# Where the memory keys' projection runs, and how the early low parts and gated attention's steps are spread

## The reference, cut to what matters

```
block 1: z = rmsnorm([meta; x]) @ w_in -> a, q, k, v, r, lr, ga, gb
         y_a = multiscale_pool(a) mixed per group @ w_pool_out
         o   = gated linear attention over chunks of 64 (q, k, v, decay from lr), normed, * silu(r)
         m   = sigmoid(ga) * y_a + sigmoid(gb) * (o @ w_gla_out);  h += m @ w_out
         h  += squared_relu(rmsnorm(h) @ w_ff1) @ w_ff2
block 2: p = rms_norm(x) @ w_in_first -> a depthwise convolution of width 31 and an 8-head
             recurrence (rwkv7), concatenated, @ w_out
         cross attention: q = h @ wq; km, vm = split(rms_norm(mem) @ wkv);  mem is 256 x 1024
         a gated MLP (w_gu, w_down)
```

## Time and profile before

| what | value |
|---|---|
| median of 3 runs | 1596.79 us |
| the profiled execution | 1598.76 us, its span 1596.9 us |
| PE busy | 1554.9 us, 97% of the span |
| DVE, ACT, POOL busy | 829.8, 648.1, 376.8 us |
| TensorE clock granted over the span | 0.992 |
| mean DMA traffic | 134 GB/s |

### The profile page before, as it was taken

How to read it: one execution, slowest core, us unless ns; L and a number is a source line. 1 busy time by engine, 2 the same in 40 slices (tenths; PEclk the granted TensorE clock), 3 DMA queues, 4 the chain that set the end, 5 groups by cost and what they waited for, 6 DMA issues and landing times.

```text
span 1596.9 us, 27596 instructions
## 1 busy us (share of the span) xinstructions
PE 1554.9 (97%) x11744; PEld 1279.7 (80%) x11744; DVE 829.8 (52%) x1290; ACT 648.1 (41%) x1019; POOL 376.8 (24%) x319
## 2 busy tenths in 40 slices
PE   8999999999999999999999988999999999999997
PEld 7887778888888888887877777779789888888877
DVE  6887523753455454545477866345427432333334
ACT  5444423443444352543465554444335322322222
POOL 0122211222011010241363251032023420330234
PEclk9999999999999999999999999999999999999999
DMA  6243212333667767634535221145122223232211
GB/s 252 84 142 113 80 54 79 111 126 134 238 245 244 256 240 264 224 108 169 199 120 185 79 105 62 56 182 187 53 80 80 81 104 106 79 106 91 94 63 70
DMA packets 49147, 213.40 MB, mean 134 GB/s; under 512 B 5248, under 2 KB 11008, under 8 KB 34048
## 3 DMA queue, kind: packets, MB, share of 16 engines
q1 hardware_dynamic: 49024, 211.63, 37.7%
HBM read 183.30 MB, written 28.31 MB: 133 GB/s over the span
## 4 chain that ended last, share of the span: by engine, by line
PE 88%; DVE 6%; issue 3%; ACT 1%; POOL 1%; DMA 0%; SPq 0%; POOLq 0%; DVEq 0%; ACTq 0%
PE ps L171 88%; DVE zf L183 2%; DVE zf L191 1%; DVE wl L183 1%; POOL zf L183 1%; DVE zr L191 1%; PE ps L174 1%; DVE ps L191 1%; ACT zf L177 1%; DVE zf L2513 0%; ACT zf L180 0%; ACT wh L180 0%; DMA wl<-lo_scratch 0%; ACT zr L180 0%; DMA zf<-in_xT 0%
## 5 line engine op out<-in xcount | busy, mean ns | idle before, releaser
L171 PE MATMUL ps<-zr,wh 128*128 128x512 f32 (+2 forms) x4028 | 1163.3, 375 | 9.6 <-ACT wh L180 5.7
L171 PEld LDWEIGHTS ps<-zr,wh 128*128 128x128 f32 x4028 | 722.8, 189 | 157.7 <-issue 7.3
L171 PE MATMUL ps<-zr,wl 128*128 128x512 f32 (+2 forms) x2008 | 742.7, 372 | 0.0
L183 POOL TENSOR_TENSOR zf<-zf 128x512 f32<-128x512 f32 (+1 forms) x230 | 271.2, 1186 | 705.3 <-ACT zf L177 478.6
L171 PEld LDWEIGHTS ps<-zr,wl 128*128 128x128 f32 x2008 | 377.7, 189 | 71.5
L183 DVE TENSOR_TENSOR wl<-raw,wh 128x1024 fp32r<-128x1024 f32 (+2 forms) x201 | 246.8, 1267 | 158.9 <-ACT wh L180 158.7
L180 ACT ACTIVATE wh<-raw 128x1024 fp32r<-128x1024 f32 (+2 forms) x243 | 240.5, 1038 | 154.9 <-PE ps L171 141.7
L177 ACT ACTIVATE zf<-zf 128x512 f32<-128x512 f32 (+2 forms) x232 | 128.0, 561 | 356.0 <-DVE zf L183 259.9
L183 DVE TENSOR_TENSOR zf<-ps,zf 128x512 f32<-128x512 f32 (+3 forms) x172 | 98.3, 578 | 178.7 <-PE ps L171 152.7
L171 PE MATMUL ps<-zf 64*64 64x64 f32 (+5 forms) x4024 | 150.7, 240 | 19.1 <-issue 8.7
L171 PEld LDWEIGHTS ps<-zf 64*64 64x64 f32 (+3 forms) x4024 | 113.2, 141 | 58.5 <-issue 41.2
(11 more groups left out here) (91 smaller groups left out, 633.3 us busy)
## 6 DMA issues: line engine op xcount, KB each, us to landing
raw<-in_wstream SPq DMA_DIRECT2D x116, 1024.0 KB, 5.3
zf<-in_wstream SPq DMA_DIRECT2D x42, 512.0 KB, 4.9
lo_scratch<-zr SPq DMA_DIRECT2D x42, 512.0 KB, 4.8
wl<-lo_scratch SPq DMA_DIRECT2D x42, 512.0 KB, 4.1
zf<-in_xT SPq DMA_DIRECT2D x16, 256.0 KB, 3.8
raw<-in_wstream SPq DMA_DIRECT2D x4, 768.0 KB, 4.3
x_scratch<-zf SPq DMA_DIRECT2D x8, 256.0 KB, 2.1
zf<-x_scratch SPq DMA_DIRECT2D x8, 256.0 KB, 4.9
```

The costliest lines, as they stand in the source:

```text
L171: return self.raw.matmul(out_, l, x, start=start, stop=stop)
L183: return self.raw.tensor_tensor(out_, a, b, o)
```

## The change

1. The four units of km move in the stream of weights from behind v to behind vm. In `schedule()` their eight tiles are gone from block 1; `bg_mem2` does them after the last packet of vm, as 32 packets of 6 matmuls (`mk`, two of a tile's eight k each), with the letter m, which `TURNS` now has 78 times for 41. `TURNS` is written anew. The normalised memory that vm is made from serves km too, so its first high and low parts (`mem.x` on ACT and DVE) go; the squares stay.
2. The four pooling mixes move among the tiles of the second unit of v.
3. `EARLY` takes km's eight pieces in and drops the two of the third unit p (the condition looks 4 units back, not 2). There are 48 pieces; piece p is read at step p, split at p + 3, and written at p + 4, so `int(1.15 * p)` is `p`.
4. Gated attention's steps: gb's tiles get rate 4 for 2. Extra empty steps: one before the scores of level 4, two before those of level 5, and more among the norms.
5. The outcome of the convolution goes to other buffers (`CR`), so it no longer waits for vm's last tile, but for the last `prep`. `wa` waits for km. The reciprocal root of the memory's norm is spread behind vm. km's results go to DRAM tile by tile (128 KB), not in pairs.

```diff
@@ unit_list
-    pair("km", "wkv_2", 0, 4)
...
     for i in range(4):
         t("vm", "wkv_2", 0, 8, (1024 + 256 * i,), 256, "M")
+    pair("km", "wkv_2", 0, 4)
@@
-EARLY = [... if u[0] in ('cv', 'vm', 'wa', 'wb', 'wq') or u[0] == "p" and UNITS[n - 2][0] in ("p", "cv")]
+EARLY = [... if u[0] in ('cv', 'vm', 'km', 'wa', 'wb', 'wq') or u[0] == "p" and UNITS[n - 4][0] in ("p", "cv")]
@@ bg_gla
+            for _ in range((4, 5, 5).count(lv)):
+                yield
...
             put("gla.sq", h)
             yield
+            if h:
+                yield
             pl.cols(f"gla.n{h}", "M")
             yield
-            if h in (0, 3):
-                yield
+            yield
@@ schedule
-            if uu == 0 and i == 2:
-                pl.spread("mem.rs")
+            if uu == 1:
+                pl.drain(bgp)
+                pl.take("M", "in.mx", i)
+                put("mix", i)
+                pl.rel("M", "in.mx", i)
         mark("v", uu)
-    pl.drain(bgp)
-    for uu in range(4):
-        n = pl.next_unit("km")
-        for j in range(2):
-            ...
-            pl.tile(n, j, 2 * uu + j)
...
-    pl.rate = 2
-    for tag, cnt in (("r", 2), ("ga", 4), ("gb", 4)):
+    for tag, cnt, pl.rate in (("r", 2, 2), ("ga", 4, 2), ("gb", 4, 4)):
@@ early
-                if int(1.15 * p) == t - 4:
+                if p == t - 4:
                     put("early.out", p)
...
-                if int(1.15 * p) == t:
+                if p == t:
                     put("early.in", p)
...
-                if int(1.15 * p) == t - 3:
+                if p == t - 3:
                     put("early", p)
@@ bg_conv
-        while not has(("vm", 3, 1)):
+        while not has(("vm", 3, 1), ("prep", 3)):
@@ bg_mem2
+        pl.spread("mem.rs", "M")
+        yield
+        for uu in range(4):
+            n = pl.next_unit("km", ahead=False)
+            pl.split(n + 1)
+            pl.load(n + 2)
+            yield
+            for j in range(2):
+                i = 2 * uu + j
+                pl.take("D", "t.km", i)
+                for k in range(0, 8, 2):
+                    put("mk", n, j, i, k, k + 2)
+                    if k == 6:
+                        put("ev.km", i)
+                        pl.rel("D", "t.km", i)
+                        mark("km", uu, j)
+                    yield
@@ bg_out
-        while not has(("conv",), ("vm", 3, 1)):
+        while not has(("conv",), ("km", 3, 1)):
@@ scalar, mem_x
-                e.cp(mem_hl(k)[0], mem_src(k), scale=vec("mem_norm_g_2", k)).then_inc(*e.up("mem.h", k))
@@ vector
-            def mem_x(k):
-                e.wait_ge(("mem.rs.sq", k))
-                lo_scaled(("mem.x", k), mem_hl(k)[1], mem_src(k), vec("mem_norm_g_2", k), mem_hl(k)[0], "mem.h", k)
```

More of the change, by code:

```diff
@@ L22 @@
 TURNS = """
[L23 to L27, removed]
+...p.pp.p.p.....pg.pgpp.g.pp.gcppcccgcgcgcpgc.gcggg.cccgcc.cpgcg.hhg.g.gcc.hgg.g.gghchc.hhcphgg.hgpc
+hgpphcc.cgcgg.g.hcp.gphpchghccg.ccmggccg..cppp.pghch.h.mphccphmphmcmphcmpcimmipmmffmpmpicicmifpmimim
+pfgciccmmcgifficmfccpmifmpmfifpgimmicmpcmgmmgccgpmcipmmpmfpmfphcmhfmgpcmmcfhpimmmificghihgcmhggigphi
+chccgmimhhfmggmmgffmccfmhgfpmmpmmhfmmgcmgchgchfpmfhpmfphmpfcpcpmfcmpmccmfmpmmfiimhifmcifhmhihcmihimc
+mciihffmfifmcmfmimfmcfcicfmoifoifiooofififfioofiifiofiofooofffffofofofoofofofofoofofooofofooooooooo
 """
@@ L113 @@
 UNITS = unit_list()
-EARLY = [n for n, u in enumerate(UNITS) if u[0] in ('cv', 'vm', 'wa', 'wb', 'wq') or u[0] == "p" and UNITS[n - 2][0] in ("p", "cv")]
+EARLY = [n for n, u in enumerate(UNITS) if u[0] in ('cv', 'vm', 'km', 'wa', 'wb', 'wq') or u[0] == "p" and UNITS[n - 4][0] in ("p", "cv")]
 PIECES = [(n, c) for n in EARLY for c in range(2)]
@@ L522, in schedule @@
                 pl.cols("mem.rs")
-            if uu == 0 and i == 2:
-                pl.spread("mem.rs")
-        mark("v", uu)
-    pl.drain(bgp)
-    for uu in range(4):
-        n = pl.next_unit("km")
-        for j in range(2):
[L530 to L533, removed]
-            pl.tile(n, j, 2 * uu + j)
+            if uu == 1:
[3 more added lines that the diff above has]
+                pl.rel("M", "in.mx", i)
+        mark("v", uu)
     for uu in range(2):
@@ L1133, in program @@
         U = sb("cu_sb", [P, NCU], u8)
-        mh = sb("mh", [P, 8, 16])
+        MR = sb("mr", [P, 256])[:, :]
+        mh, sm, km16 = MR[:, 0:128].rearrange("p (k t) -> p k t", t=16), MR[:, 128:192], MR[:, 192:256]
         msq = sb("msq", [P, 16])
         mrs = sb("mrs", [P, 16])
-        sm = sb("sm", [P, 64])
-        km16 = sb("km16", [P, 64])
         x_raw_m = mh
@@ L1243, in program @@
         ACC, TMP, RSTD, TMP2 = F(66), F(67), F(68), F(69)
-        RA, MR = F(63), F(38)[:, 256:512]
+        RA = F(63)
         cu_raw, pmx = F(55, NCU), F(54)
@@ L1256, in program @@
         mraw = F(0, 2048)
-        kv_out = [F(73), F(74), F(50)]
+        km_out = [F(40)[:, 0:256], F(40)[:, 256:512]]
         vm_out = [F(51)[:, 256:512], F(40)[:, 0:256]]
@@ L1283, in program @@
         ZC = [F(47, 2168)[:, 542 * i:542 * (i + 1)] for i in range(4)]
-        CS = [64, 44, 22, 23]
+        CS, CR = [64, 44, 22, 23], [38, 39, 49, 50]
         CO, CP = [F(i) for i in CS], F(58)
@@ L1324, in cat_hl @@
         def cat_hl(i):
-            return R(CS[i]), R(47 + i)
+            return R(CS[i]), R(CR[i])
         def prep_bufs(hp):
@@ L1437, in operand @@
                 return R(RO[k]), R(VS[k]), ("fin.out", k)
-            if tag == "km":
-                return (*mem_hl(k), ("mem.x", k))
-            if tag == "vm":
+            if tag in ("vm", "km"):
                 return (*mem2_hl(k), ("mem.x2", k))
@@ L1500, in mm, with mk @@
                 for k in range(nk // 2) if half == 0 else range(nk // 2, nk):
-                    dense(n, j, ps(*K), k, operand(tag, i, k), 256 if tag == "km" else 512, K)
+                    dense(n, j, ps(*K), k, operand(tag, i, k), 512, K)
+            def mk(n, j, i, k0, k1):
+                K = ("t.km", i)
+                if k0 == 0:
+                    e.wait_ge(freed(*K))
+                for k in range(k0, k1):
+                    dense(n, j, ps(*K), k, operand("km", i, k), 256, K)
             def part(n, j, i, k, h):
@@ L1589, in ko @@
                         e.wait_ge(freed(*K))
-                    dense(n, j, ps(*K), k, operand(tag, i0 + j, k), 256 if tag == "km" else 512, K)
+                    dense(n, j, ps(*K), k, operand(tag, i0 + j, k), 512, K)
             def rows(n, i, name, k0=0, k1=8):
@@ L1972, in tensor @@
             run(e, {
-                "mm": mm, "idle": idle, "lr": lr, "mw": mw, "kw": kw, "kt": kt, "ko": ko, "mh": mh, "koh": koh, "rows": rows, "cols": cols, "spread": spread, "gla.gate": gla_gate,
+                "mm": mm, "idle": idle, "lr": lr, "mw": mw, "kw": kw, "kt": kt, "ko": ko, "mh": mh, "koh": koh, "mk": mk, "rows": rows, "cols": cols, "spread": spread, "gla.gate": gla_gate,
                 "gla.score": gla_score, "gla.turn": gla_turn, "gla.turnm": gla_turnm, "gla.state0": gla_state0,
@@ L2268, in cat @@
                 e.wait_ge(("conv.res", i))
-                e.cp(cat_hl(i)[0], F(47 + i)).then_inc(*e.up("cat.h", i))
+                e.cp(cat_hl(i)[0], F(CR[i])).then_inc(*e.up("cat.h", i))
             def ev_wa(i):
@@ L2658, in conv_out @@
             def conv_out(i):
-                e.wait_ge(("conv.sg", i), ("conv.x", i), ("mm", "t.vm", pl.base["vm"][3], 1))
-                e.stt(F(47 + i), CO[i], vec("conv_ln_b_2", i), F(45 + i % 2), ADD, MUL).then_inc(*e.up("conv.res", i))
+                e.wait_ge(("conv.sg", i), ("conv.x", i))
+                e.stt(F(CR[i]), CO[i], vec("conv_ln_b_2", i), F(45 + i % 2), ADD, MUL).then_inc(*e.up("conv.res", i))
             def pset():
@@ L2816, in cat @@
             def cat(i):
-                lo(("cat", i), cat_hl(i)[1], F(47 + i), cat_hl(i)[0], "cat.h", i)
+                lo(("cat", i), cat_hl(i)[1], F(CR[i]), cat_hl(i)[0], "cat.h", i)
             def ev_wb(i):
@@ L2826, in evh_wb @@
                 e.tt(half(YS[i], h), half(ps("t.wb", i), h), half(WP[i], h), ADD).then_inc(*e.up(*K))
-            def mem_x(k):
-                e.wait_ge(("mem.rs.sq", k))
-                lo_scaled(("mem.x", k), mem_hl(k)[1], mem_src(k), vec("mem_norm_g_2", k), mem_hl(k)[0], "mem.h", k)
             def mem_x2(k):
                 lo_scaled(("mem.x2", k), mem2_hl(k)[1], mem2_src(k), vec("mem_norm_g_2", k), mem2_hl(k)[0], "mem.h2", k)
[L2835 to L2839, removed]
             def ev_km(i):
-                e.wait_ge(("mm", "t.km", i), ("mem.rs.s",))
-                e.tt(kv_tile(i), ps("t.km", i)[:, 0:256], MR, MUL).then_inc(*e.up("t.km", i))
+                e.wait_ge(("mm", "t.km", i), ("mem.rs.s",), ("kv.out", i // 2 - 1, i % 2) if i >= 2 else ("kv.out", 7, 1) if i == 0 else None)
+                e.tt(km_out[i % 2], ps("t.km", i)[:, 0:256], MR, MUL).then_inc(*e.up("t.km", i))
             def ev_vm(n, mt):
@@ L2925, in vector @@
```

(12 more changed lines are left out.)

5 lines of the change are left out of this document (removed).

## The result

The changed kernel takes 1658.49 us (median of 4 runs, 1654.70 to 1665.13), the one before 1597.14 us beside it: ratio 1.0377 (1.0357 to 1.0397), slower. The forecast was 1645 in a range of 1614 to 1675. The profiled execution took 1654.7 us, its span 1652.9, which is 56.0 more than the span before. The medians lie 61.4 us apart and the spans 56.0: the profiled execution was the shortest of the four, and the 5.4 us between the two are in no trace (the heads' stage scatters by as much, see the end).

What follows compares the result with a forecast made beforehand. It took PE, busy 97% of the span, as the bound. PE's waits for late weights, +64 us, less 15.5 us from block 1 and the heads, gave +48.5 us on 1596.9: 1645 us, range 1614 to 1675.

Steps and rivals of the forecast that it cites:

- The queue's slip: Feed-forward stretch, SyncE's queue: 14.8 us a trip pair against PE's 11.2, slipping 77 us over 43 trips.
- The first rival: SyncE's queue keeps pace with PE, leaving only block 1 and the heads: 1581 us; chance 12%.
- What covers it: Feed-forward weights: 12.9 us of slack covers part of the slip, leaving 64 us of PE waits; nothing added for evictions.
- Block 1: Without km, -26 us from v to f1 and -1 ahead of v; together -27, bounds -29 and -24.
- the removed wait at level 5: Block 1, gated attention: extra steps give POOL time, so its 1.62 us wait before level 5 goes.
- The wait for the last norm: Block 1: the last norm is nearer to the unit go, costing 0 to 1.5 us, 0.5 taken.
- the states and output steps: Block 1: last state and first output step have no tile between; PE waits 1 to 2 us, 1.5 taken.
- The heads: Heads' stage with km: +25.5 us of work, 14 us absorbed, so +11.5; bounds +3.5 and +21.5.
- The third unit p: Its low parts are made on DVE again, 2 x 1.22 us beside 11 us of matmuls: 0, at most +2.
- The queue keeps pace: Rival: steady trips pipeline better or writes aren't held by loads; only block 1 and heads count: 1581 us; 12%.
- The packets delay the heads: Rival: the slip comes as forecast, nothing is absorbed, and packets push chains back: +65, 1662 us; 14%.
- A partial slip: Rival: trip pairs of 13 us in SyncE's queue give 26 us, less 15.5: 1607 us; 6%.

Runs made afterwards that it cites:

- e2: The changed kernel with each early read issued one step later, all 48 pieces kept; 1590.49 us, ratio 0.9952 to the kernel before.
- e3: The kernel before with only `int(1.15 * p)` replaced by `p`, still 42 pieces; 1654.05 us, ratio 1.0338 to the kernel before.
- e7: e6 with the empty step ahead of gated attention's level 4 moved behind level 6; 1590.90 us, ratio 0.9942 to the kernel before.
- e6: e2 without the empty step behind each of the last three squares of gated attention's norms; 1590.95 us, ratio 0.9946 to the kernel before.
- e5: e2 leaving out the products of 6 of the 8 weight blocks of each km tile; 1587.34 us, ratio 0.9923 to the kernel before.
- e1: The changed kernel with the old 42 early pieces at `int(1.15 * p)`, km's low parts made on VectorE in the heads; 1602.24 us, ratio 1.0018 to the kernel before.
- e4: e2 with one empty step fewer ahead of gated attention's level 4; 1594.00 us, ratio 0.9956 to the kernel before.

## Why the prediction was right, point by point

**The queue's slip: right in place, mechanism and nearly in size.** The first shared read (piece 4) was issued at 389.87 us and the last (piece 47) at 702.28: 312.4 us for 43 trips, 14.53 us a pair, which was the forecast's low end (14.8 taken). The tiles they belong to are 240.8 us of work, so the queue slipped 71.6 us, not 77. e2 shows that the chain is the cause, e3 that the spacing makes most of it by itself. The first rival argued from bandwidth; e2's 272 GB/s show that the bandwidth was there, and the chain did not use it. The estimate of 11.2 us a pair, worked out from the Trainium skill ("DMA: Bandwidth & Descriptors", "Anatomy of one DMA — SWDGE (gpsimd) path"), isn't what this trace shows (14.53). The limit of about 358 GB/s that the Trainium skill gives on the same page ("Specifications") was not reached, in e2 neither.

Two rows were misread, and no term hangs on either. The wait of 5.7 us is not that of the first unit p: PE stands from 0 to 5.68 us, ahead of the kernel's first matmul, before and after the change alike. And the pair of 415.40 to 429.93 us is not one trip with a load and one without: a second load was issued at 424.71, behind the write.

**What covers it: the term that failed.** "Evictions queue behind the late split [...] so I add nothing for that" is refuted, though it cost less than PE's waits suggest. At the last unit for which PE waited for weights it had lost 61.2 us in all (its place among the stage's matmuls, against the trace before), so 10.4 of the queue's 71.6 us were covered, for 12.9 forecast. The other 5.2 us of the 66.3 came behind it. At each of the last three turns from f1 to f2 (the group before them had no loss yet) PE stood 3.4 us in a wait for POOL's low parts of the activations, 10.2 us together. Behind the first two of them PE caught up with the queue and waited for weights again (until 523.70 and 625.53 us), so they lay within the queue's slip. Behind the third there is no late weight any more, and its 3.4 us and the lower clock that followed were lost for good. The last wait for weights, and the third for POOL:

```profile
712.23 0.71 PE L171 MATMUL ps<-zr,wh 128*128 128x512 f32 x2 [1.15 <-issue]
```

```profile
720.97 0.73 PE L171 MATMUL ps<-zr,wh 128*128 128x512 f32 x2 [3.39 <-POOL zr L183]
```

How such a wait comes about, at the first of the three: VectorE's work ahead of it, and then PE's own row (columns as above):

```profile
478.44 2.36 DVE L183 TENSOR_TENSOR wl<-raw,wh 128x1024 fp32r<-128x1024 f32 x2 [2.73 <-ACT wh L180]
480.71 0.68 DVE L191 SCALAR_TENSOR_TENSOR zf<-ps,zf 128x512 f32<-128x512 f32 x1
483.71 1.48 DVE L183 TENSOR_TENSOR zr<-zf,zr 128x1024 fp32r<-128x1024 f32 x1 [2.31 <-ACT zr L180]
485.11 0.68 DVE L191 SCALAR_TENSOR_TENSOR zf<-ps,zf 128x512 f32<-128x512 f32 x1
```

```profile
488.51 1.22 PE L171 MATMUL ps<-zr,wh 128*128 128x512 f32 x2 [3.39 <-POOL zr L183]
```

The eviction at 480.71 is that of a tile which PE had ended at 473.4; it stood behind the splits of a unit whose load had come late. The next, of a tile ended at 479.0, began at 485.11, behind it and an early piece whose own high part waits on ScalarE behind that eviction's activation. From there the low part is 3.4 us away, and PE stood them. So it isn't enough that a late weight and the eviction are late at the same time: each holds the other up. The errors nearly cancel: 5.4 us too much slip, against 2.5 us too much cover and 5.2 us at the end that the forecast put at nothing. So 64 against 66.3 is a better hit than the steps earned. The lower clock behind PE's waits, 15.9 us in 250, is no further term as long as PE waits for the queue again: the queue's time was longer than PE's, at either level. Only behind the last wait does it count, with 1.6 of the 5.2 us.

**Block 1: -19.8 for -26.** The km tiles went as forecast; the removed wait at level 5 did not. It was to go (-1.6), and has become 2.68 us, and 3.4 us at the lower clock behind it. PE of the changed kernel in order of time (start, us, what, idle before):

```profile
164.95 0.39 PE L171 MATMUL ps<-zr,wl 128*128 128x512 f32 x1
168.02 0.69 PE L171 MATMUL ps<-zf 64*64 64x64 f32 x32 [2.68 <-issue]
168.64 0.72 PE L171 MATMUL ps<-zr,wh 128*128 128x512 f32 x2
...
169.44 1.05 PE L171 MATMUL ps<-zr,wh 128*128 128x512 f32 x2
...
172.00 1.01 PE L171 MATMUL ps<-zr,wh 128*128 128x512 f32 x2
```

The profile puts it down to "issue"; what the score step needs are POOL's two products of level 5. In the row of three below they are the last two, behind one of the unit ga; they and VectorE's two weight splits ran beside each other. POOL, then VectorE:

```profile
161.86 6.06 POOL L183 TENSOR_TENSOR zf<-zf 128x512 f32<-128x512 f32 x3 [3.06 <-ACT zf L177]
```

```profile
162.77 4.03 DVE L183 TENSOR_TENSOR wl<-raw,wh 128x1024 fp32r<-128x1024 f32 x2 [0.45 <-ACT wh L180]
```

One by one in the trace, the two products take 2.27 and 2.25 us and end at 167.9, where PE goes on; the splits take 1.80 and 2.30 us, where the earlier trace rows have 1.22. The forecast saw that the extra steps give POOL time; it didn't see that they move the level onto the splits of a unit. The Trainium skill's "SBUF — State Buffer", section "Who interferes with whom", says that a VectorE instruction with two inputs in SBUF contends with a GpSimd one that reads SBUF, and that the order of issue decides which of the two blocks. The trace agrees that both come out longer; which blocked which can't be seen in it. e7 moves the levels by a step and is 4.9 us shorter from v to f1 than the changed kernel, of which e6 has 2.4; its split comes behind the products, which take 1.75 us each:

```profile
162.39 4.71 POOL L183 TENSOR_TENSOR zf<-zf 128x512 f32<-128x512 f32 x3 [9.21 <-ACT zf L177]
```

The wait for the last norm, put at 0.5 us, was 2.4 (go's first tile), and e6 takes it away. Two smaller ones add to it: the rows tiles behind three of the mixes took 0.3 us each more than their like, and the first po tile 2.2 us more, since VectorE's evictions stood behind one another there (PE goes on at 92.54, 93.59 and 94.64 us, each time as one of them ends). Against them, the states and output steps were to take 1.5 us more and took 1.4 less, two states to a half tile, with the wait ahead of the first output step at 0.9 us.

**The heads: +10.2 for +11.5, and this is luck in part.** That packets fill waits is shown by e5. But with the same steps the stage took 445.7 to 454.0 us in five runs, mean 449.7, which is 14 us over the 435.5 before (e3, with the old steps, took 436.6): the forecast is within that scatter, and so would be 6 us more. The profiled execution of the changed kernel has the shortest of the five. The third unit p was taken at 0 (at most +2) for two low parts on VectorE; e1 warns that such work can cost its whole length in the heads; no run took it alone.

**The rivals.** "The queue keeps pace" (1581 us) fell by the trips, 14.53 us a pair, and not for want of bandwidth: e2, where it does keep pace, took 1590.49. Of the 9.5 us above that rival's sum 2.5 are the kernel before, 1599.60 us in this comparison for 1597, and the rest is block 1, 18.6 us shorter in e2 for the 26 forecast. "The packets delay the heads" fell at e5. "A partial slip" fell with the slip itself.

**What stays open.** The heads' stage scatters by 4 us either way with one step order. The clock goes with it: in the order of the stage's time, 445.7 (after), 447.4 (e2), 450.0 (e6), 451.2 (e7) and 454.0 us (e4), the lower level was granted for 10.2, 13.6, 20.4, 17.0 and 23.8 us of it (mean granted clock 0.99 in the first, 0.97 in the last). At half the clock, 13.6 us more of it are 6.8 of the 8.3 us between the first and the last. These stretches, 3.4 or 6.8 us long, fall on different steps from run to run (in the one before at 882.0, 940.0, 977.6, 987.8 and 1076.6 us). Why they do isn't settled, and with one trace of each kernel neither is whether the clock makes the longer waits or follows them.

## What to carry to other kernels

When a queue that issues in order waits for the landing of a write, look at what is issued right ahead of that wait: if write and wait fall into one step, the queue runs one landing at a time, whatever bandwidth is left, and a step between them takes the loss away (66 us here). Pick such trips out of the trace of before, where a few of them stand in a row, and multiply; a DMA share or a GB/s figure would have said that there is room. Work moved among chains that PE takes part in fills waits if it is PE's (most of 16.8 us were free), and costs about its length if it is that of the other engine in the chains (8.4 us of VectorE's, 7.8 us).

## What the runs showed of the hardware

- A read issued behind the landing of the write ahead of it took 5.64 us a trip in the mean with 1 MB in it (22 trips, 5.17 to 6.11), and 8.97 us with 2 MB (21 trips, 8.18 to 11.78). At e2's 272 GB/s the bytes alone are 3.9 and 7.7 us, an estimate: the other 1.8 and 1.3 us a trip are what waiting for the landing costs. The median landing of the same 512 KB write was 7.3 us in the changed kernel, issued right behind a read and often a load, and 3.6 us in e2, issued ahead of them:

```profile
lo_scratch<-zr SPq DMA_DIRECT2D x43, 512.0 KB, 3.6
```

- In block 1 and the feed-forward stage of the changed kernel each of PE's eleven waits of 2.7 to 5.0 us brought 3.4 or 6.8 us at the lower clock level (1.05 us for two matmuls of 512 columns in place of 0.63), and none of its waits of up to 1.2 us did. Before the change the feed-forward stage had neither. In the heads it is less regular: a wait of 3.05 us was followed by none, one of 1.58 us (before, at 987.75) by 3.4 us.
- VectorE's 1024-wide subtraction out of SBUF, 1.22 us alone, took 1.80 and 2.30 us beside POOL's products of 512, and those went from 1.29 us alone (1.75 beside VectorE's own products) to 2.27.
